# Reading the weight rows of a down projection in seven column orders

## The reference

```python
def reference(x, meta_tokens, norm1_g, w_in, ...):
    ...
    for l in range(DEPTH):
        xn = _rmsnorm(h, norm1_g[l])
        proj = xn @ w_in[l]
        ...
        mix = (jax.nn.sigmoid(g_a + gbias[:D_MODEL]) * ya
               + jax.nn.sigmoid(g_b + gbias[D_MODEL:2 * D_MODEL]) * yb
               + jax.nn.sigmoid(g_c + gbias[2 * D_MODEL:]) * yc)
        h = h + mix @ w_o[l]

        u = _causal_dwconv(_rmsnorm(h, norm2_g[l]) @ w_up[l], mlp_conv_w[l])
        u_gate, u_up = jnp.split(u, 2, axis=-1)
        h = h + (jax.nn.silu(u_gate) * u_up) @ w_down[l]
    return _rmsnorm(h, final_norm_g)[:, N_META:]
```

## Time and profile before

| | |
|---|---|
| median of the runs | 1746.43 us |
| profiled execution, its span | 1745.1 us |
| TensorE busy with matmuls | 1734.3 us, 99% |
| VectorE busy | 1117.8 us, 64% |
| ScalarE busy | 763.7 us, 44% |
| down projection, first to last matmul | 1492.9 to 1737.0 us |

### The profile page before, as it was taken

One profiled execution on the slowest core, in us unless ns is written; L12 is line 12 of the kernel. 1 busy time (PEld: TensorE's weight loads), 2 busy tenths in 40 slices (PEclk: granted clock), 3 DMA queues, 4 the chain that ended last, 5 costly groups with the idle time before them and its releaser, 6 DMA issues.

```text
span 1745.1 us, 34098 instructions
## 1 busy us (share of the span) xinstructions
PE 1734.3 (99%) x13429; PEld 1680.7 (96%) x13429; DVE 1117.8 (64%) x1607; ACT 763.7 (44%) x921; POOL 263.3 (15%) x494
## 2 busy tenths in 40 slices
PE   9999999999999999999999999999999999999998
PEld 8999999999999999999999999999999999888886
DVE  6857766667565554555556687777777777554454
ACT  6635444354354444444444444334444444343433
POOL 3153332630530000000000043321000000000000
PEclk9999999999999999999999999999999999999999
DMA  8567557666565655556645566666555565665654
GB/s 232 169 180 186 168 149 198 176 175 178 153 184 181 189 178 178 175 182 194 201 159 192 181 195 192 204 200 192 183 182 181 180 186 180 223 190 189 189 192 134
DMA packets 310296, 320.62 MB, mean 184 GB/s; under 512 B 17353, under 2 KB 285133, under 8 KB 310093
## 3 DMA queue, kind: packets, MB, share of 16 engines
q1 hardware_dynamic: 296861, 311.01, 58.2%
q0 software_dynamic: 12928, 7.80, 2.0%
q10 hardware_dynamic: 432, 0.79, 0.1%
HBM read 311.10 MB, written 2.11 MB: 179 GB/s over the span
## 4 chain that ended last, share of the span: by engine, by line
PE 99%; DVE 0%; DMA 0%; ACT 0%; SPq 0%; issue 0%; ACTq 0%; DVEq 0%
PE ps L1435 27%; PE ps L1437 27%; PE ps L1436 27%; PE ps L1693 5%; PE ps L1692 5%; PE ps L1691 5%; PE ps L1526 0%; DMA xb<-in_x_dram 0%; PE ps L1540 0%; PE ps L1565 0%; PE ps L1555 0%; PE ps L1556 0%; PE ps L1584 0%; PE ps L1585 0%; DVE xl L941 0%; DVE lo L896 0%
## 5 line engine op out<-in xcount | busy, mean ns | idle before, releaser
L896 DVE TENSOR_TENSOR lo<-raw,hi 128x1024 fp32r<-128x1024 f32 x584 | 709.9, 1229 | 494.4 <-ACT hi L627 490.2
L1435 PE MATMUL ps<-xh,hi 128*128 128x260 f32 (+1 forms) x3328 | 945.8, 284 | 0.2 <-DVE xl L941 0.2
L1437 PE MATMUL ps<-xh,lo 128*128 128x260 f32 (+1 forms) x3328 | 941.7, 283 | 0.0
L1436 PE MATMUL ps<-xl,hi 128*128 128x260 f32 (+1 forms) x3328 | 936.5, 281 | 0.0
L627 ACT CAST hi<-raw 128x1024 fp32r<-128x1024 f32 x584 | 604.8, 1048 | 671.8 <-PE ps L1437 539.0
L1436 PEld LDWEIGHTS ps<-xl,hi 128*128 128x128 f32 x3328 | 626.6, 188 | 0.2
L1435 PEld LDWEIGHTS ps<-xh,hi 128*128 128x128 f32 x3328 | 625.2, 188 | 1.3 <-issue 0.4
L1437 PEld LDWEIGHTS ps<-xh,lo 128*128 128x128 f32 x3328 | 624.7, 188 | 0.0
L610 POOL DMA_DIRECT2D hT<-h2b x128 | 69.6, 553 | 604.3 <-DVE h2b L1289 599.7
L1693 PE MATMUL ps<-lo,act_h 128*128 128x512 f32 x350 | 138.5, 396 | 0.0
L1692 PE MATMUL ps<-hi,act_l 128*128 128x512 f32 x350 | 137.3, 392 | 0.0
(11 more groups left out here) (298 smaller groups left out, 1383.6 us busy)
## 6 DMA issues: line engine op xcount, KB each, us to landing
raw<-in_w_in_dram SPq DMA_DIRECT2D x224, 512.0 KB, 3.6
raw<-in_w_up_dram SPq DMA_DIRECT2D x176, 512.0 KB, 4.6
raw<-in_w_down_dram SPq DMA_DIRECT2D x88, 512.0 KB, 4.7
raw<-in_w_o_dram SPq DMA_DIRECT2D x32, 512.0 KB, 3.4
raw<-in_w_in_dram SPq DMA_DIRECT2D x32, 256.0 KB, 4.2
raw<-in_w_a_o_dram SPq DMA_DIRECT2D x16, 512.0 KB, 4.3
raw<-in_w_b_o_dram SPq DMA_DIRECT2D x16, 512.0 KB, 3.3
raw<-in_w_c_o_dram SPq DMA_DIRECT2D x16, 512.0 KB, 3.3
```

The lines of the kernel that those rows point to most:

```text
L896: nc.vector.tensor_tensor(part(ph, i, q, lo_all), raw[:, s, :], part(ph, i, q, hi_all).bitcast(F32), ALU.subtract).then_inc(lo_ready, 1)
L1435: nc.tensor.matmul(acc, w_hi, mh, start=first and j == 0, stop=False)
L1436: nc.tensor.matmul(acc, w_hi, ml, start=False, stop=False)
L1437: ins = nc.tensor.matmul(acc, w_lo, mh, start=False, stop=last and j == KJ - 1)
```

## The change

A table `RUNS` gives each group and each block of the down projection an order in which the 512 columns of a weight row are read. An entry (pieces, run) takes `run` columns from each of `pieces` equal parts of the row in turn; (None, 2) takes the even columns first, then the odd ones; (1, 512) is the row as it lies. So:

- group 0: block 0 in runs of 4 from two halves, block 1 in runs of 16 from two halves
- group 1: block 0 in runs of 2 from two halves, block 1 even columns first
- group 2: block 0 in runs of 8 from two halves, block 1 in runs of 4 from four quarters
- group 3: as before

The moving operand of each matmul is read through that view (`as_streamed`), the result lies in PSUM in the order read, and VectorE's addition puts it back by reading PSUM through the opposite view (`as_written`); the residual is read and written contiguously. The stationary operand, the output of each matmul, the loads, the rounding and the splitting are untouched. Row by row, the instructions of each engine stand in the same order as before, with the same waits and semaphores and the same counts; only line numbers and these access patterns differ, so no list of them is shown.

```diff
@@
 DAT, DPAD = 4, 128
+RUNS = (((2, 4), (2, 16)), ((2, 2), (None, 2)), ((2, 8), (4, 4)), ((1, 512), (1, 512)))
@@
+        def as_streamed(row, g, b):
+
+            pieces, run = RUNS[g][b]
+            if pieces is None:
+                return row.rearrange("p (n r) -> p r n", r=run)
+            return row.rearrange("p (h n r) -> p n h r", h=pieces, r=run)
+
+        def as_written(acc, g, b):
+
+            pieces, run = RUNS[g][b]
+            if pieces is None:
+                return acc.rearrange("p (r n) -> p n r", r=run)
+            return acc.rearrange("p (n h r) -> p h n r", h=pieces, r=run)
+
+        def as_columns(row, g, b):
+
+            pieces, run = RUNS[g][b]
+            if pieces is None:
+                return row.rearrange("p (n r) -> p n r", r=run)
+            return row.rearrange("p (h n r) -> p h n r", h=pieces, r=run)
@@
                         for b in range(2):
-                            nc.vector.tensor_tensor(ybuf[:, g, b, :], ybuf[:, g, b, :], ps[:, 2 * (g % 2) + b, :],
+                            own = as_columns(ybuf[:, g, b, :], g, b)
+                            nc.vector.tensor_tensor(own, own, as_written(ps[:, 2 * (g % 2) + b, :], g, b),
                                                     ALU.add).then_inc(set_free[g % 2], 1)
@@
             def down_rows(i, q, b, last=False):
-                st = (i * 2 + q // DQ) % 2
+                g = i * 2 + q // DQ
+                st = g % 2
                 for j in range(DK):
                     kt = (q % DQ) * DK + j
-                    w_hi, w_lo = streamed(i, q, hi_all)[:, j, :], streamed(i, q, lo_all)[:, j, :]
+                    w_hi, w_lo = (as_streamed(streamed(i, q, buf)[:, j, :], g, b) for buf in (hi_all, lo_all))
```

## The result

The changed kernel takes 1798.9 us (two runs, 1798.75 and 1799.06) against 1746.43: a ratio of 1.0297, with a 95% interval of 1.0281 to 1.0314. The profiled execution has a span of 1797.2 us, 52.1 more than before. The forecast was 1806.6 us; the change was to cost 60.2 us and cost 52.1 us of the span.

What follows compares the result with a forecast made beforehand. TensorE's matmul pace was taken to bound the kernel. Two terms of +30.1 us in group 1, the rest 0, gave 60.2 us on a 1745.1 us span, plus 1.3 us from span to median: 1806.6 us, range 1742 to 1812.

Steps and rivals of the forecast that it cites:

- the case of no difference: Rival for the changed matmuls: TensorE's reader overlaps accesses, so the time stays, 1746 us (1742 to 1751); chance 0.24.
- the prediction's own signs: Windows by group: group 1 takes 121 us instead of 61, the others stay at 61; groups 0 and 2 past 63 mean hops cost.
- The bound, and that nothing else moves: Whole kernel: TensorE is busy 99% of the span, so a change counts only through the pace of its matmuls.
- the cover of VectorE and ScalarE: Down projection groups, about 61 us each: VectorE is busy 29 to 31 us and ScalarE 23 to 26, leaving half to spare.
- The additions: Six VectorE additions reading PSUM in pieces: one alternates word by word, 0.35 us more, off the path; taken as 0.
- Even columns first: Group 1, block 1, 132 matmuls: two of four words per pass, 256 accesses instead of 128; +30.1 us.
- Runs of 2 from two halves: Group 1, block 0, 132 matmuls: each 16-byte piece visited twice, 459 ns instead of 231; +30.1 us.
- Runs of 4, 8 and 16: Both blocks of groups 0 and 2, 528 matmuls: whole 16-byte pieces in another order, no price for hops; taken as 0.
- the upper bound of 31.9 us: Groups 0 and 2: every run start exposes 0.69 ns, +31.9 us in all; as the rival that every hop costs, chance 0.13.
- The flat rows of VectorE: VectorE at L1014: runs of two or more words cost nothing extra at 1.03 ns a column, so hops were priced at 0.
- The reading of the 6%: fp32r matmuls run 6% under the array's pace because supply of the moving operand limits them, 231.2 against 213.3 ns.
- The rival "a gain": All 792 changed matmuls: hopping between halves avoids a conflict between neighbouring pieces, at most 14.2 us, about 1738 us; chance 0.05.

## Why the prediction was right, and where it wasn't

The forecast was 1806.6 us, and 1803 to 1808 if its mechanism was right; 1798.9 lies below both. The direction, the bound and one of the two large terms were right. The wide range, 1742 to 1812, holds the result because it also took in the case of no difference. By the prediction's own signs group 1 should have taken 121 us (103.1 measured), and groups 0 and 2 over 63 us meant that hops cost (65.0 and 67.3).

**The bound, and that nothing else moves: right.** TensorE's pace alone set the change, the cover of VectorE and ScalarE held, and the difference is matmuls times pace within 0.3 us. The additions cost nothing, less than the 0.35 us allowed: PSUM read word by word from two places has no price on VectorE.

**Even columns first: the size right, the picture in part.** Forecast 459 ns and +30.1 us, measured 451.4 and +29.1. Plain fp32 at every 4th column, 1.76 ns a piece, shows the price itself, which the forecast had taken from 4 x 0.445 = 1.78 and from VectorE's 1.72. But the forecast had one reader with one access at a time, and every 4th column would then take 911 ns; it takes 460. That one reader and two readers both give 256 accesses in a row for the even columns is luck. The Trainium skill's rule of two hits on a line (page "SBUF — State Buffer", section "SBUF: two separate sides"), weighed in the prediction as the rival of no change, fails here when the hits are counted over the stream: two words used of 16 bytes per visit ran at half speed in every form but runs of 2 from halves. Counted for each of the two readers it nearly holds: contiguous rows give a reader two words of each piece and take 7% longer than an order with four, even columns give it one and take 2.1 times as long. In plain fp32 two words fall short by 5% (449.5 against 429 ns); four are enough there.

**Runs of 2 from two halves: the term that was mis-sized.** Forecast +228 ns a matmul, +30.1 us; measured +98.5 ns, +13.0 us. The step "each 16-byte piece is visited twice, 256 accesses in place of 128" holds for runs of 2 from 4, 8, 16, 64 and 128 pieces (447 to 487 ns) and not for two halves. Theory C alone doesn't give this exception: each reader changes the piece at each of its words there, 451 ns. Starts off the mark showed the same exception for runs of 4 from two halves (330 to 333) and not from quarters (443 to 480). The cause stays open. That a reader keeps two pieces at hand fits in direction only: it would give 231 ns for runs of 2 from two halves (330 measured) and 216 for single words from quarters (274 measured), it leaves the 330 to 333 of runs of 4 off the mark unexplained, where at least one of the readers goes through four pieces in turn and the last two are never the next, and the plain fp32 pass has 453 from two halves.

**Runs of 4, 8 and 16: taken at 0, measured +21, +13, +9 and, from quarters, +35 ns**: 10.3 us together, a third of the upper bound of 31.9 us. The flat rows of VectorE didn't carry over. The two errors, -17.1 and +10.3 us, cancelled in part: that 60.2 forecast and 52.1 measured lie so near is partly luck. The price depends on the distance of the pieces; by what rule stays open.

**The reading of the 6%: right in kind, incomplete.** It is supply; a quarter of the weight columns gave back 2 ns of it. But the forecast had one reader that needs all four words of a piece. The runs behave as if there were two, and contiguous rows are slow because each of them has to fetch every piece for two of its words: 128 x 1.76 = 225 ns and 2.5 fixed make 228, and by their start they take 227 to 236. What makes the difference between starts stays open. The rival "a gain" had a ceiling of 17.9 ns a matmul, of which 15.4 were reached, and its mechanism was wrong: hopping by runs never gave more than 1 ns, single words in turns between two places did.

## What to carry to other kernels

Where fp32r matmuls follow each other at 0.45 ns a column with the clock granted, let the moving operand alternate word by word between two places, near or far, and put the columns back when PSUM is read. Stretches of 8 words are enough if they start on a multiple of 16 bytes; two halves of the row may start 8 bytes off it (216.3 ns). It is worth 15.4 ns, or 6.7%, of a matmul of 512 columns. An order that gives a reader a new 16 bytes for two of its own words loses that again (contiguous rows 227 to 236 ns, runs of 4 and more that start on a multiple of 16 bytes 230 to 281), and one that does so for a single word takes twice as long (433 to 487 ns); the exceptions are runs of 2 from two halves (330), runs of 4 from two halves off the mark (330 to 333) and single words from quarters (274).

## What the runs showed of the hardware

- A full-rate fp32r matmul takes the even and the odd places of its moving stream as if through two readers. Each gets an aligned 16 bytes in about 1.76 ns: single words in turns from stretches of 8 words 215.6 ns, from stretches of 4 words 232.4, and the same stretches of 8 words started 8 bytes off 232.2.
- 215.8 ns for 512 columns is 213.3 at 2.4 GHz and 2.5 more; contiguous rows have 227 to 236, by their start. The 215.7 ns that the Trainium skill gives on the page "TensorE: Matmul & The Clock Gate", section "Wait — 56ns, not 53.3ns?", is met by fp32r too, but here only by single words in turns from two halves or from the two parts of stretches of 8, 16 or 32 words.
- Hops of 256 bytes are the dearest: single words and runs of 2 from 8 pieces 486.7 ns, every 64th column 487.0, runs of 4 from 8 pieces 280.9. Why is open.
- A plain fp32 pass takes a word every 0.83 ns and behaves as one reader: 429 ns contiguous, 449.5 with two words used of 16 bytes, 900 with one.
- 258 columns in turns go at 111.8 ns where the columns alone would have 110. That this is the weight load beside them was expected from the plain fp32 matmuls of 64 columns in the branches, which are 112 ns apart, and was not tried.
